# Scaling of the mixer's attention and SSD rows, and the first convolution tap, on ScalarE instead of VectorE

## The reference

```
proj = h @ w_in                      # h = RMSNorm(x); q, k, v, z, xBC, dt
attn = rms_norm(sliding_window_attention(rope(q), rope(k), v, sinks), attn_out_norm_w)
xbc  = silu(conv_b + sum_j conv_w[j] * xbc[t - 3 + j])         # causal depthwise, 4 taps
y    = ssd_chunked(xs, dt, a, B, C) + d_skip * xs              # 32 chunks of 128 tokens
g    = y * silu(z)
ssd  = g * rsqrt(mean(g * g, per half of 256) + eps) * ssd_out_norm_w
x    = x + concat([attn, ssd], -1) @ w_out
```

## Time and profile before

| | us |
|---|---|
| median of 3 runs (2225.43 to 2232.58) | 2231.68 |
| the profiled execution | 2244.56 |
| span of its slowest core (core 7) | 2243.5 |
| spans of the other cores | 2197.9 to 2225.1 |
| mean granted PE clock, core 7 | 0.827 |

### The profile page before, as it was taken

One profiled execution on the slowest core, in us unless ns is written; L12 is line 12 of the kernel. 1 busy time (PEld: TensorE's weight loads), 2 busy tenths in 40 slices (PEclk: granted clock), 3 DMA queues, 4 the chain that ended last, 5 costly groups with the idle time before them and its releaser, 6 DMA issues.

```text
span 2243.5 us, 29573 instructions; the slowest of 8 cores (2197.9 to 2243.5 us)
## 1 busy us (share of the span) xinstructions
PE 1558.4 (69%) x8686; PEld 789.9 (35%) x8686; DVE 1300.0 (58%) x2479; ACT 970.7 (43%) x1837; POOL 932.4 (42%) x1104
## 2 busy tenths in 40 slices
PE   0467686776768686867267777777457777877786
PEld 0233343333334343433145455555322232332332
DVE  2448567574847576756244554544346666666676
ACT  2346355454535353533254544544124444444453
POOL 0125445363535454434201100111246766776676
PEclk9889798888888797968677766777578989898898
DMA  7535454454545354445834342311166777877520
GB/s 193 165 90 119 97 113 106 113 97 117 92 118 92 104 95 113 76 94 96 173 103 132 115 139 76 117 71 75 38 210 214 256 247 265 275 243 268 196 93 1
DMA packets 95300, 302.86 MB, mean 135 GB/s; under 512 B 24200, under 2 KB 26376, under 8 KB 91696
## 3 DMA queue, kind: packets, MB, share of 16 engines
q0 software_dynamic: 53488, 138.65, 26.9%
q1 hardware_dynamic: 41664, 162.32, 21.8%
HBM read 401.67 MB, written 143.79 MB: 243 GB/s over the span
## 4 chain that ended last, share of the span: by engine, by line
PE 26%; DVE 21%; DMA 15%; issue 13%; POOL 12%; ACT 11%; another core or an unknown queue 1%; SPq 1%; POOLq 0%; DVEq 0%; ACTq 0%
PE pst L337 22%; ACT arena L310 8%; DVE arena L313 8%; DVE arena L324 6%; DVE arena L317 5%; POOL arena L313 4%; DMA arena<-x 4%; PE pst L348 4%; POOL arena L1455 3%; DMA wbscr<-we 3%; POOL out L1462 2%; DMA arena<-out,arena 2%; ACT arena L329 1%; DMA arena<-x2scr 1%; DVE arena L320 1%
## 5 line engine op out<-in xcount | busy, mean ns | idle before, releaser
L337 PE MATMUL pst<-arena 128*128 128x512 bf16 (+12 forms) x6373 | 1366.3, 358 | 358.2 <-ACT arena L310 92.7
L337 PEld LDWEIGHTS pst<-arena 128*128 128x128 bf16 (+2 forms) x6373 | 610.2, 124 | 1055.4 <-issue 516.2
L310 ACT ACTIVATE arena<-arena 128x1 f32<-128x1 f32 (+7 forms) x589 | 399.1, 701 | 579.2 <-DVE arena L324 212.6
L313 POOL TENSOR_TENSOR arena<-arena 128x1 f32<-128x1 f32 (+6 forms) x399 | 388.3, 982 | 307.5 <-DVE arena L313 149.1
L348 PE MATMUL pst<-arena 128*128 128x128 bf16 (+1 forms) x2313 | 251.4, 257 | 316.1 <-ACT arena L310 145.6
L310 ACT ACTIVATE arena<-pst 128x512 bf16<-128x512 f32 (+3 forms) x557 | 293.5, 547 | 320.5 <-PE pst L337 204.5
L313 DVE TENSOR_TENSOR arena<-pst,arena 128x512 f32<-128x512 f32 (+4 forms) x490 | 265.6, 558 | 235.0 <-PE pst L337 178.2
L329 ACT ACTIVATE arena<-pst 128x256 bf16<-128x256 bf16 (+3 forms) x334 | 227.2, 716 | 293.3 <-PE pst L348 238.9
L324 DVE SCALAR_TENSOR_TENSOR arena<-arena 128x512 f32<-128x512 f32 (+6 forms) x371 | 335.1, 911 | 17.9 <-ACT arena L310 8.7
L348 PEld LDWEIGHTS pst<-arena 128*128 128x128 bf16 (+1 forms) x2313 | 192.9, 119 | 386.6 <-ACT arena L310 127.3
L1291 POOL DMA_INDIRECT slots<-arena x64 | 63.6, 994 | 458.8 <-DVE arena L331 443.7
(11 more groups left out here) (23 smaller groups left out, 281.8 us busy)
## 6 DMA issues: line engine op xcount, KB each, us to landing
arena<-wbscr SPq DMA_DIRECT2D x90, 1536.0 KB, 9.9
wbscr<-we POOLq DMA_DIRECT2D x96, 512.0 KB, 5.6
arena<-x SPq DMA_DIRECT2D x64, 512.0 KB, 5.8
x2scr<-arena SPq DMA_DIRECT2D x32, 512.0 KB, 3.0
arena<-x2scr SPq DMA_DIRECT2D x32, 512.0 KB, 7.1
out<-arena SPq DMA_DIRECT2D x32, 512.0 KB, 3.1
xnscr<-arena SPq DMA_DIRECT2D x32, 256.0 KB
arena<-wbscr SPq DMA_DIRECT2D x15, 512.0 KB, 5.8
```

Source lines behind the costliest of these rows:

```text
L310: S.op("act", lambda e: e.activation(out=out, in_=in_, func=func, **kw), R, W, cost=c)
L313: S.op(eng, lambda e: e.tensor_tensor(out=out, in0=in0, in1=in1, op=op), R, W, cost=ecost(eng, out))
L337: i = e.matmul(o, lhsT=l, rhs=r, start=st, stop=sp)
```

## The change

Three kinds of steps move from DVE to ACT, with the same operands and results: the first convolution tap (8 blocks per supertile), the scaling of the attention rows (4 per supertile) and of the SSD rows (8 halves per supertile). Each becomes an ACTIVATE with Copy and a scale column, which `a1_gen` already uses for its norm. Over the mixer these are 64, 32 and 64 instructions.

```diff
@@ conv_gen
-            ts("dve", ac, xp[:, 0:512], cols[:, C_CONVW + c * 4:C_CONVW + c * 4 + 1], None, ALU.mult, None,
-               [kxp, "cols"], [kac])
+            act(ac, xp[:, 0:512], AF.Copy, [kxp, "cols"], [kac], scale=cols[:, C_CONVW + c * 4:C_CONVW + c * 4 + 1])
@@ swa_gen
-            ts("dve", mix[j % 2][:, 0:512], attn, rsc, None, ALU.mult, None, ["attn", "swrs"], ["mixA%d" % (j % 2)])
+            act(mix[j % 2][:, 0:512], attn, AF.Copy, ["attn", "swrs"], ["mixA%d" % (j % 2)], scale=rsc)
@@ ssdT_gen
             for g in range(2):
-                ts("dve", mix[j % 2][:, 512 + g * 256:512 + (g + 1) * 256], y1f[:, g * 256:(g + 1) * 256],
-                   smA[:, 14 + g:15 + g], None, ALU.mult, None, ["y1", "sdrs"], ["mixB%d" % (j % 2)])
+                act(mix[j % 2][:, 512 + g * 256:512 + (g + 1) * 256], y1f[:, g * 256:(g + 1) * 256], AF.Copy,
+                    ["y1", "sdrs"], ["mixB%d" % (j % 2)], scale=smA[:, 14 + g:15 + g])
```

## The result

The changed kernel takes 2196.86 us (median of 4 runs, 2192.63 to 2208.64) against 2229.27 (median of 4 runs, 2225.43 to 2232.58): ratio 0.9864, 95% interval 0.9821 to 0.9906. The forecast was 2198. The profiled execution took 2192.63 us; it is shown on core 1.

What follows compares the result with a forecast made beforehand. The mixer was taken as bound by handoffs between engines, PE and DVE fullest. Gains of 4.4, 1.2 and 0.7 us per supertile, two thirds arriving, give 34 us over eight: 2231.68 to about 2198 us, range 2163 to 2240.

Steps and rivals of the forecast that it cites:

- What bounds it: Mixer bound by work handed between engines, PE and DVE fullest; later phases unchanged; a supertile falls from 122 to 118 us.
- Prices of the moved steps: ACT steps priced flat, not stretched by POOL: 711 ns for 512 columns, 508 for 256.
- DVE's busy time: In the mixer the moved steps take 122.8 us off DVE, 15.3 per supertile.
- The sum: Gain per supertile: 4.4 us at 434 to 462 us, 1.2 at 488, 0.7 at the end, together 6.3.
- (c): End of a supertile: scalings of 2.47 us before the output transpose become 1.7 on ACT, gain 0.7 us.
- The two thirds: Of 6.3 us per supertile 4.2 arrive, 34 us over eight; the rest goes to waits now second.
- What would have shown it wrong: Wrong if POOL disturbs ACT's steps, or the new order moves an x load or weight transfer onto the chain.
- Rival B: POOL's chain steps, freed of DVE's long scalings, shrink a quarter and all 6.3 us arrive: 2168 us; chance 0.15.
- Rival C: POOL's disturbance moves to DVE's multiply-adds, 3.1 us of excess stays per supertile: 2215 us; chance 0.15.
- Rival D: Loads of x and PE set the pace; only 0.7 us at each supertile's end comes through: 2226 us; chance 0.12.
- Rival E: Scalings on ACT wait for POOL's reciprocal root, delaying PSUM copies and exponentials PE needs: 2248 us; chance 0.18.

Runs made afterwards that it cites:

- micro program: Program of its own, mixer left out: 24 DVE or ACT steps of 512 columns, alone and beside POOL products; ACT Copy 721 ns alone, 722 beside POOL.
- e5: Order of the kernel before the change, but all three kinds of steps issued on ACT; ratio 0.9976 against before, mixer end +4.0 us.
- e4: Changed kernel's order, but all three kinds of steps issued on DVE as before; ratio 1.0084 against the kernel before, mixer end +18.6 us.

## Why the prediction came out right, and where its steps did not

- **What bounds it.** Right. The later phases gave nothing, PE stayed at 87 to 89 us per supertile, and a middle period fell from some 122 to 117 us (118 was forecast).
- **Prices of the moved steps.** Right: 0.506, 0.713 and 0.72 us against 0.508 and 0.711. That ACT is not stretched by POOL was a choice; the micro program shows it (721, 722).
- **DVE's busy time.** 136.7 us less instead of 122.8. The excess of 14 us is in steps that stayed: DVE's 64 bf16 products of 512 columns fell from 1066 to 781 ns, 18 us. That they met POOL less is the likely reason, and was not shown.
- **The sum.** 6.3 us per supertile, 8 x 6.3 = 50.4 us in full, was worked out from rows of the old order, and there it did not come: with the same steps on ACT in that order (e5) the mixer ends 4.0 us later. In the order of after the engine brings 50.3 us (+18.6 to -31.7). That this is the number of the sum is chance. The sum priced four of the eight taps of a supertile. By kind it had 3.20 - 0.71 = 2.5 us of taps, 20 us in all, and 3.8 us of scalings, some 30 us, where the runs show 28.7 and 21.6. The taps were mis-sized low by 9 us, the scalings high by 9, and the errors cancelled. One term can be seen by itself: (c), 0.7 us, came as 0.8.
- **The two thirds.** The step that failed. "The other third is given back to waits that are now second" gave 34 us where 31.7 came, so its size held, but its cause did not. In one fixed order the engine's gain is not two thirds of the sum: it is nothing in the old order and all of the sum's number in the new one. The prediction counted the new order as nothing in its forecast and had it only as an aside, in D and E, as a case in which the change does not do what it says. The runs show that it costs 18.6 us with the steps on DVE and brings 35.7 with them on ACT. So 50.4 - 18.6 = 31.8 us, which would be the forecast with e4's number in hand, is one of two ways to split the gain; by the other, the engine brings nothing and the order all.
- **What would have shown it wrong.** One of the signs that the prediction named did come: the new order put a load of x behind others on SP, and DVE waits for it (some 6 us in up to five supertiles). "SP's transfers keep their order at the end of a supertile" is right for the end, but in the middle of five supertiles they changed places.
- **Rival B** (all of 6.3 us arrive and POOL's steps shrink as well, 2168): did not come. POOL was not freed: its busy time is 936.2 us, against 932.4 in the earlier trace rows.
- **Rival C** (the disturbance moves to the multiply-adds): its premise holds, the micro program doubles them (752 to 1577 ns). In the kernel it did not decide: 873 ns against 853, and e4, with the taps still on DVE in the same order, has 874. So the rise of 20 ns belongs to the order, and the multiply-adds last as long behind a tap on ACT as behind one on DVE.
- **Rival D** (hidden behind the loads of x): the loads of x have 11.8% of 116 us on the chain, 13.7 us; before they had 12.4% of 101, 12.5 us. They did not hide the gain. But 8.6 us of the loads of `trigtab` came onto the chain beside them, as told under e4.
- **Rival E** (ACT's queue behind the root): the mechanism is real. ACT's wait for POOL grew by 37.7 us and PE's for ACT before a matmul by 34.2. Against it, PE's waits before the transposes fell from 93.8 + 37.0 to 69.5 us, by 61.3; about half of that is there already in e4 (89.0 + 11.1 us), so it comes with the order. In the old order (e5) the rise was the same and the fall only 42.6, and no gain was left. E needed three places of eight per supertile where PE waits 2.05 us more, 8 x 3 x 2.05 = 49 us; 34.2 came, and not all of it from scalings.

## What to carry to other kernels

Where a planner makes the order, moving a step to another engine is two changes. Measure them apart: book the step on one engine and issue it on the other, in both combinations. Here the engine was worth -50 us in the new order and nothing in the old, and the order +19 with the steps on DVE and -36 with them on ACT: a gain of this kind has no share that belongs to one of the two, and a price read in the old order says little of the new one. Compare the streams of the transfers too, though no transfer was touched: here a load that changed places makes DVE wait some 6 us in up to five supertiles. A step that waits for a third engine is harmless or harmful on a queue by what stands right behind it. Where calls are drained, choose per call: the better of two orders in each call ended the mixer ahead of both (-44.2 us against -31.7 and -28.6).

## What the runs showed of the hardware

That a DVE step beside a POOL product does not slow down by a share but takes turns with it, one for one, was not expected: 486 ns became 2.45 us and 752 ns 2.70. Both lose nearly the same, 1.96 and 1.95 us. POOL's product of 1024 columns, 2.42 us alone, hardly loses beside the DVE product (2.46) and 0.28 us beside the multiply-add (2.70). So the loss of the DVE step is near the length of POOL's and doesn't go by its own. Whether it shrinks in step with a shorter POOL product was not run; POOL's steps of one column hold nothing.
